# Memory attention with the decode tile second, other engine orders in the window phase, and output projections whose first three tiles are rounded by feature slice

## What is computed

```python
h = x + jnp.concatenate([out_a, out_b, out_c], axis=-1) @ lw['w_o']
h = h + memory_attend(rmsnorm(h, lw['norm_mem_g']), mem_k, mem_v, lw)

def memory_attend(hn, mem_k, mem_v, lw):
    q = rmsnorm((hn @ lw['w_mq']).reshape(B, T, MEM_HEADS, MEM_HD), lw['mem_q_norm_g'])
    s = jnp.einsum('bqhd,bkhd->bhqk', q, mem_k) * (MEM_HD ** -0.5)
    p = jax.nn.softmax(s, axis=-1)
    return jnp.einsum('bhqk,bkhd->bqhd', p, mem_v).reshape(B, T, D_MODEL) @ lw['w_mo']
```

## Time and profile before

| | us |
|---|---|
| median of the runs | 1981.98 |
| profiled execution, own time | 1981.09 |
| its span | 1979.6 |
| TensorE busy (PE) | 1853.4, 94% |
| weight loads (PEld) | 1697.4, 86% |
| VectorE busy (DVE) | 1140.2, 58% |
| ScalarE busy (ACT) | 787.6, 40% |
| GpSimd busy (POOL) | 739.6, 37% |

### The profile page before, as it was taken

How to read it: one execution, slowest core, us unless ns; L and a number is a source line. 1 busy time by engine, 2 the same in 40 slices (tenths; PEclk the granted TensorE clock), 3 DMA queues, 4 the chain that set the end, 5 groups by cost and what they waited for, 6 DMA issues and landing times. The chain is left out here.

```text
span 1979.6 us, 27880 instructions
## 1 busy us (share of the span) xinstructions
PE 1853.4 (94%) x10427; PEld 1697.4 (86%) x10427; DVE 1140.2 (58%) x1348; ACT 787.6 (40%) x1483; POOL 739.6 (37%) x652
## 2 busy tenths in 40 slices
PE   5999999989979799898997997999999999999999
PEld 4989889989958587898985786999999999988787
DVE  4225555856655511521341217887887887699995
ACT  4115663325675421411401316444444444444432
POOL 3001212015534240221201503766666666546743
PEclk9999999999989899998998998999999999999999
DMA  5111211232144230212053212222222222386544
GB/s 161 35 55 47 55 33 45 81 111 86 57 142 152 87 126 1 64 64 86 1 182 114 87 44 82 67 67 77 76 67 67 77 66 76 133 325 210 177 165 153
DMA packets 159033, 188.07 MB, mean 95 GB/s; under 512 B 13809, under 2 KB 112730, under 8 KB 158520
## 3 DMA queue, kind: packets, MB, share of 16 engines
q1 hardware_dynamic: 157156, 186.30, 28.6%
q10 hardware_dynamic: 884, 0.25, 0.1%
q0 software_dynamic: 896, 0.19, 0.1%
HBM read 151.64 MB, written 35.07 MB: 94 GB/s over the span
## 5 line engine op out<-in xcount | busy, mean ns | idle before, releaser
L3394 PE MATMUL ffn_banks<-h_parts,up_hi 128*128 128x384 f32 x1936 | 495.8, 337 | 11.5 <-POOL h_parts L3793 4.3
L3394 PEld LDWEIGHTS ffn_banks<-h_parts,up_hi 128*128 128x128 f32 x1936 | 351.6, 189 | 13.5 <-issue 8.2
L3394 PE MATMUL ffn_banks<-h_parts,up_lo 128*128 128x384 f32 x968 | 325.0, 336 | 0.0
L3789 POOL TENSOR_TENSOR up_lo<-up_raw,up_hi 128x512 fp32r<-128x512 f32 x176 | 256.7, 1474 | 139.1 <-ACT up_hi L3547 139.1
L761 PE MATMUL proj_banks<-x_hi,in_w_hi 128*128 128x384 f32 (+1 forms) x648 | 223.4, 345 | 4.2 <-DVE room L1148 4.2
L761 PE MATMUL proj_banks<-x_hi,in_w_lo 128*128 128x384 f32 (+1 forms) x648 | 218.2, 337 | 0.0
L761 PE MATMUL proj_banks<-x_lo,in_w_hi 128*128 128x384 f32 (+1 forms) x648 | 218.1, 337 | 0.0
L3394 PEld LDWEIGHTS ffn_banks<-h_parts,up_lo 128*128 128x128 f32 x968 | 183.0, 189 | 0.0
L3840 POOL TENSOR_TENSOR h_parts<-down_cells,h_parts 128x512 fp32r<-128x512 f32 x69 | 110.9, 1614 | 89.7 <-ACT h_parts L3620 89.6
L3510 PE MATMUL ffn_banks<-h_parts,up_hi 128*128 128x512 f32 x352 | 138.3, 393 | 2.5 <-DVE h L4067 1.9
L3513 PE MATMUL ffn_banks<-h_parts,up_lo 128*128 128x512 f32 x352 | 137.1, 390 | 0.0
(11 more groups left out here) (470 smaller groups left out, 3900.3 us busy)
## 6 DMA issues: line engine op xcount, KB each, us to landing
up_raw<-in_w_up SPq DMA_DIRECT2D x44, 512.0 KB, 3.8
down_cells<-in_w_down SPq DMA_DIRECT2D x58, 256.0 KB, 5.5
up_raw<-ffn_gated_rows SPq DMA_DIRECT2D x44, 320.0 KB, 5.3
ffn_gated_rows<-h SPq DMA_DIRECT2D x22, 576.0 KB
in_w_raw<-in_w_in SPq DMA_DIRECT2D x24, 512.0 KB, 3.7
up_raw<-ffn_gated_rows SPq DMA_DIRECT2D x44, 256.0 KB, 3.2
mem_k_one<-in_cache_mem_k SPq DMA_DIRECT2D x8, 1024.0 KB, 4.9
spill<-mixT SPq DMA_DIRECT2D x10, 576.0 KB, 3.8
```

Source lines behind the costliest of these rows:

```text
L3394: ins = nc.tensor.matmul(banks[:, bank, 0:TC], wt[:, j, k, :], parts[:, q, x, k, :], start=(fresh and n == 1), stop=(n == last), skip_grou ...
L3789: nc.gpsimd.tensor_tensor(w_lo[:, j], weights.full(j), w_hi[:, j].bitcast(F32), ALU.subtract).then_inc(weights.split[j], 1)
```

## The change

Three parts. Nothing is computed otherwise; instructions and waits change their places and sizes.

1. Window phase: the orders of VectorE and ScalarE. One load of ScalarE's function table goes, the copy of the transposed values stands behind the scaling of the memory rows, `exponentials(0)` behind the first two high parts, `maxima(1)` ahead of `weights_low(3)`, `copy_turned(0)` and `weights_high(3)` ahead of `exponentials(1)`, `weights_high(4)` behind `rows_out(0)`. The key lengths are inverted at i = 3, and the eight normalizations are spread over i = 3, 4 and 5.

```diff
 LENGTHS_AT = {1: (0, 1), 2: (2,), 3: (3,)}
-KEYS_AT = {5: (0, 1, 2, 3), 6: (4, 5, 6, 7)}
+FACTORS_AT = 3
+KEYS_AT = {3: (0, 1), 4: (2, 3, 4), 5: (5, 6, 7)}
...
             nc.vector.tensor_copy(k_rows[:], t_bank[:, 1:3, :]).then_inc(rows_copied, 1)
+            for f in range(2):
+                low(f)
             denominators(0)
-            for f in range(4):
-                low(f)
-            for f in range(4, KD):
+            for f in range(2, KD):
                 low(f)
             weights_low(1)
+            maxima(1)
             weights_low(3)
-            maxima(1)
             denominators(1)
...
-                if i == 4:
+                if i == FACTORS_AT:
                     refine_keys()
                 for n in KEYS_AT.get(i, ()):
...
-            nc.scalar.preload_act_table_set("natural_log_exp_and_others")
-            act.wait_ge(v_turned, 1)
-            nc.scalar.activation(v_rows[:, 0:8, :], t_bank, ACT.Copy).then_inc(v_copied, 1)
...
+            act.wait_ge(v_turned, 1)
+            nc.scalar.activation(v_rows[:, 0:8, :], t_bank, ACT.Copy).then_inc(v_copied, 1)
+            for f in range(2):
+                high(f)
             exponentials(0)
-            for f in range(4):
+            for f in range(2, 4):
                 high(f)
             weights_high(0)
             for f in range(4, KD):
                 high(f)
-            for j in range(1, 4):
+            for j in range(1, 3):
                 weights_high(j)
+            copy_turned(0)
+            weights_high(3)
             exponentials(1)
-            for j in range(4, PAIRS_FIRST):
-                weights_high(j)
             for i in range(NT):
-                copy_turned(i)
-                if i == 0:
+                if i:
+                    copy_turned(i)
+                else:
                     rows_out(0)
+                    weights_high(PAIRS_FIRST - 1)
                 for g in LENGTHS_AT.get(i, ()):
                     key_lengths(g)
                 for j in PAIRS_AT.get(i, ()):
                     weights_high(j)
                 if i + 2 < NT:
                     exponentials(i + 2)
-                if i == 4:
+                if i == FACTORS_AT:
                     key_factors()
```

```diff
...
-            sp.wait_ge(w_split, i - self.RING + 1)
+            sp.wait_ge(w_split, i - self.RING + 2)
...
-            for k in range(KD):
-                pe.wait_ge(w_split, k + 1)
+            pe.wait_ge(act_high_first, 1)
+            for half in range(2):
+                for a, w in ((a_hi, w_hi), (a_lo, w_hi), (a_hi, w_lo)):
+                    if w is w_lo:
+                        pe.wait_ge(w_split, half + 1)
+                    elif a is a_hi:
+                        pe.wait_ge(w_high, half + 1)
+                    elif half == 0:
+                        pe.wait_ge(act_split_first, 1)
+                    for t in range(together):
+                        nc.tensor.matmul(banks[:, 2 * t + half, :], a[:, t, 0, :], half_of(w[:, 0], half),
+                                         start=(a is a_hi and w is w_hi), stop=False)
+            for k in range(1, KD):
+                pe.wait_ge(w_split, k + 2)
+                pe.wait_ge(act_split_first, k + 1)
                 for n in range(2 * together):
-                    if k == 0 and n % 2 == 0:
-                        pe.wait_ge(act_split_first, n // 2 + 1)
                     products(n, k)
...
-            for k in range(KD):
+            nc.scalar.activation(a_hi[:, 0:together, 0], first_slice(0), ACT.Copy).then_inc(act_high_first, 1)
+            weights.wait(act, 0)
+            for half in range(2):
+                nc.scalar.activation(half_of(w_hi[:, 0], half), half_of(weights.at(0), half), ACT.Copy).then_inc(w_high, 1)
+            for k in range(1, KD):
+                nc.scalar.activation(a_hi[:, 0:together, k], first_slice(k), ACT.Copy).then_inc(act_high_first, 1)
                 weights.wait(act, k)
                 nc.scalar.activation(w_hi[:, k], weights.at(k), ACT.Copy).then_inc(w_high, 1)
-                if k < together:
-                    act_hi_part(k)
...
-            pool.wait_ge(w_split, 1)
+            pool.wait_ge(w_split, 2)
             for k in range(1, KD):
-                pool.wait_ge(w_high, k + 1)
+                pool.wait_ge(w_high, k + 2)
...
-                pool.wait_ge(act_high, t + 1)
+                pool.wait_ge(act_high, t - together + 1)
...
-            dve.wait_ge(w_high, 1)
-            nc.vector.tensor_tensor(w_lo[:, 0], weights.at(0), w_hi[:, 0].bitcast(F32), ALU.subtract).then_inc(w_split, 1)
-            for t in range(together):
-                dve.wait_ge(act_high, t + 1)
-                nc.vector.tensor_tensor(a_lo[:, t], act_tile(t), a_hi[:, t].bitcast(F32), ALU.subtract
-                                        ).then_inc(act_split_first, 1)
+            def low_slice(k):
+                dve.wait_ge(act_high_first, k + 1)
+                nc.vector.tensor_tensor(a_lo[:, 0:together, k], first_slice(k), a_hi[:, 0:together, k].bitcast(F32),
+                                        ALU.subtract).then_inc(act_split_first, 1)
+
+            low_slice(0)
+            for half in range(2):
+                dve.wait_ge(w_high, half + 1)
+                nc.vector.tensor_tensor(half_of(w_lo[:, 0], half), half_of(weights.at(0), half),
+                                        half_of(w_hi[:, 0], half).bitcast(F32), ALU.subtract).then_inc(w_split, 1)
+            for k in range(1, KD):
+                low_slice(k)
```

```diff
+    last = NT - 1
+    SAMPLE_AT = 1
+    tile_at = [0, last] + list(range(1, last))
...
+            for b in range(4):
+                load_k(b)
+            for b in range(2):
+                load_v(b)
+            for b in range(4, NB):
+                load_k(b)
+            for b in range(2, NB):
+                load_v(b)
+            load_next(sp)
...
+            def sample_scores(out):
+
+                for m in range(HEADS * NB + 2):
+                    if m >= 2:
+                        b, h = divmod(m - 2, HEADS)
+                        pe.wait_ge(masked_ready, b + 1)
+                        pe.wait_ge(k_copied, m - 1)
+                        for j in range(2):
+                            ins = nc.tensor.matmul(out[:, h, :], masked[:, b % 2, 2 * h + j, :], k_one_t[:, m % 2, j, :],
+                                                   start=(b == 0 and h % 2 == 0 and j == 0), stop=(b == NB - 1 and j == 1),
+                                                   skip_group_check=True)
+                        ins.then_inc(k_used, 1)
+                    if m < HEADS * NB:
+                        b, h = divmod(m, HEADS)
+                        if h == 0:
+                            pe.wait_ge(k_landed[b % 2], 16 * (b // 2 + 1))
+                        if m >= 2:
+                            pe.wait_ge(k_copied, m - 1)
+                        for j in range(2):
+                            for kt in range(2):
+                                ins = nc.tensor.transpose(o_bank[:, 4 * (m % 2) + 2 * j + kt, :],
+                                                          k_one[:, b % 2, kt, P * (2 * h + j):P * (2 * h + j) + P], C.ident[:])
+                        ins.then_inc(k_turned, 1)
...
+            def turn_rows():
+
+                pe.wait_ge(rows_copied, 1)
+                for f in range(8):
+                    ins = nc.tensor.transpose(o_bank[:, f, :], rows[:, P * f:P * f + P], C.ident[:])
+                ins.then_inc(rows_turned, 1)
...
+            def output(i):
+                t, now = tile_at[i], pT[:, i % 2]
+                if i:
+                    pe.wait_ge(out_copied, i)
                 else:
+                    pe.wait_ge(k_copied, HEADS * NB)
...
+            score(0)
+            score(1)
+            for i in range(NT):
+                turn(i)
+                if i == SAMPLE_AT + 1:
+                    turn_rows()
+                if i + 2 < NT:
+                    score(i + 2)
+                output(i)
...
+            def copy_keys():
+
+                for m in range(HEADS * NB):
+                    if m == HEADS:
+                        denominators(0)
...
+            maxima(0)
+            copy_keys()
+            maxima(1)
+            for i in range(NT):
+                if i == SAMPLE_AT + 1:
+                    copy_rows()
+                if i + 1 < NT:
+                    denominators(i + 1)
+                if i:
+                    output_copy(i - 1)
+                if i + 2 < NT:
+                    maxima(i + 2)
+            output_copy(NT - 1)
...
+                if i == SAMPLE_AT + 2:
+                    act.wait_ge(rows_turned, 1)
...
+            exponentials(0)
+            for i in range(NT):
+                if i + 1 < NT:
+                    exponentials(i + 1)
+                copy_turned(i)
...
+            for n in range(2):
+                mask(n, qT[:, :, TP:T])
+            normalize(0)
```

(9 more changed lines are left out.)

471 lines of the change are left out of this document (159 added, 312 removed).

## The result

The changed kernel takes 1946.59 us (median, 1945.3 to 1949.46) against 1982.17 for the kernel before: ratio 0.9823 (95% interval 0.9806 to 0.984), 35.6 us less by the medians, 35.1 by the ratio (3.4 either way). The forecast was 1946. The profiled execution took 1945.3 us, its span is 1943.8 us, against 1981.09 and 1979.6 before; no product was added or taken out, and TensorE's busy time fell by 11.3 us all the same, so what went is idle time and half clock. First the busy lines of the page and then the stages; after each stretch stand its length, the busy times of TensorE, its weight loads, VectorE, ScalarE and GpSimd with their counts, TensorE's granted clock, the DMA share and GB/s.

A forecast was written before the change was run, and what follows sets the result against it. TensorE was taken as the bound, busy nearly everywhere, so only its pauses and half clock could be won: 2.0 + 7.2 + 6.0 + 17.6 + 5.8 - 2.9 = 35.7 us, giving 1946 us, range 1938 to 1957.

The forecast's parts named there:

- window phase, start: Start of window phase: unit 8 sooner, new 3.8 us pause before `turn(1)`; gain 3.5 us, taken as 2.0, bounds 0 and 7.3.
- window phase, end: End of window phase: 0.8 us of the first pause, the 5.10 us pause and 2.0 us half clock go; 7.2 us.
- first projection: Start of the first output projection: first product about 1.3 us after ScalarE's start; gain 6.0 us before clock.
- memory attention: Memory attention: pauses and half clock worth 21.2 us go, new waits of 1.4, 0.3, 1.5 and 0.4; gain 17.6 us.
- second projection: Start of the second output projection: 7.7 us lost before, new loss 1.9; gain 5.8 us before clock.
- clock behind the projections' pauses: Output projections: one of the two starts is hit by half clock behind its new pause, costing 2.9 us.
- GpSimd's order and its first release are as before: Window phase start: early edits cost nothing, covered by GpSimd; units 0 to 7 still end at 587.86.
- the stall of 0.5 us at slice 1: Output projection start: weight slice 1 ready 6.0 us in but wanted at 5.5, so TensorE stalls 0.5 us.
- The split into waits and clock: Memory attention: gain divided into vanished waits (4.05, 6.12, 1.70 us among them) and avoided half clock (2.6 and 3.8 us).
- The rival of half clock in the key steps: Memory attention: key steps and value products take up to twice as long, 70 us more, 2016; chance 0.02.
- That with no new pause caught by the clock: All new pauses: none brings half clock, 3.5 instead of 2.0 at window start, no 2.9; 40.1 us, 1942; chance 0.20.
- the late keys: Attention part of a rival: value loads hold keys 4 to 6; with late window copies 8 to 13 us back; chance 0.13.

The follow-up runs named there:

- cache copy early: Changed kernel with VectorE's copy of the transposed window cache ahead of the low part of weight pair 7 instead of behind it: 1946.54 us, ratio 0.9814.
- all filled: Changed kernel plus early cache copy, tile 0 exponentials first, value loads behind keys 0 and 1, and dummy transposes in TensorE's pauses: 1939.64 us, ratio 0.9793.

## Why the prediction was right, step by step

Forecast and measured, in us; the measured ones are differences of the two profiled executions, 35.8 in all:

| term | forecast | measured |
|---|---|---|
| window phase, start | 2.0 | -0.7 |
| window phase, end | 7.2 | 6.3 |
| first projection | 6.0, less clock | 5.0 |
| memory attention | 17.6 | 17.8 |
| second projection | 5.8, less clock | 5.6 |
| clock behind the projections' pauses | -2.9 | in the two above |
| elsewhere | 0 | 1.9 |
| sum | 35.7 | 35.8 |

- **Window phase, start: the step that failed** is "GpSimd's order and its first release are as before". The exponentials of tile 0 now stood behind two high parts, the first of which waited 2.5 us for TensorE; GpSimd's first normalization came 1.1 us later from the phase's start (11.77 us in, before 10.64). It took both the new order and the longer half clock at the phase's start to make it late (above). With the exponentials put back, units 0 to 7 end 23.1 us into the phase, exactly where the earlier trace rows has them (587.86), and `turn(1)` starts 34.9 us in, where the forecast said 599.8, 35.0 us in. So the forecast's gain of 3.5 us was to be had; 1.5 us went with the late release, and 2.8 with half clock behind `turn(1)`, for which it had allowed 1.5. The pause itself, 3.2 us for 3.8, hides a second gap: nothing was taken for VectorE's steps that GpSimd held up (last section), among them the low part of pair 5, 3.4 us instead of 1.2. The low part of pair 7 itself cost the 1.2 us it was priced at. In after the held-up VectorE came to it only 0.3 us late, because pair 7 was rounded late as well (at 598.87, forecast 597.35); with the cache copy ahead of pair 7, the copy stands behind these held-up steps, and 2.08 us of pause are left.
- **Window phase, end:** mechanism and place right. The first pause shrank by 0.4 instead of 0.8 us, since the three normalizations that stand ahead of the copy take 2.9 us; the 5.10 us one went, one of 1.0 us took its place at 666.67 (the text of the forecast says 0.5, its sum takes 0.7). No copy near output 4 came late: from 613.47 to 660.00 TensorE never paused.
- **Projections:** the first product comes 1.7 and 1.5 us into the phase (1.8 and 1.6 forecast), and from there TensorE does not pause: the stall of 0.5 us at slice 1 did not come. Half clock stood behind one of the two starts, as taken, but it cost 1.3 us (C-D is 106.0 us in after and 104.7 in the runs where the clock held) and not 2.9: it lasted 3.5 us, from 679.4 to 682.9, and not the 6.8 that were taken. Without it the first projection's gain is 6.3 us.
- **Attention:** the new waits are within 0.1 us of the forecast: 1.40 for key 4 (1.5), 0.44 and a run of 1.09 for `turn_rows` (1.4 together), 0.33 for `output(2)` (0.3), 1.40 after the first transposes (1.3). The key steps, for which nothing was taken, stay at 1.30 us. The split into waits and clock was tried alone and held: 5.95 us against 6.4. The rival of half clock in the key steps is out: clock 1.00 from 911.8 to the end.
- **Elsewhere, not forecast:** the query projection, 125.84 to 123.85 us. It ends with 36 matmuls one column wide, and nearly the whole difference is in them, 6.14 us before and 4.30 after:

```profile
913.10 6.14 PE L2795 MATMUL mq_sums<-ones,mq_squares 128*128 128x1 f32 x36
902.92 4.30 PE L2592 MATMUL mq_sums<-ones,mq_squares 128*128 128x1 f32 x36
```

Before, the clock fell 2.1 us after the first of them, at 915.2, while TensorE was busy; after, 5.2 us after it, at 908.1, with the phase's end. In all 14 traces it fell 2.1 to 5.5 us after the first of these matmuls. So these 2 us are no gain of the change. The theory that the attention brings them fails as a rule: with the new attention the clock fell early as well, 2.7 and 3.0 us in (cache copy early, all filled), and D-E was 126.8 and 124.4. With the old one it fell 2.1 to 3.2 us in, five times of five; whether that is more than chance stays open. The forecast had half clock only behind pauses, and this stretch is one without.

That the sum came out to 0.1 us is therefore chance in part: misses of 2.7 and 0.9 us in the window phase were made up by 1.9 us that came unasked elsewhere and 1.7 us at the projections, where half clock had been priced too high. Of the rivals none came about in after. That with no new pause caught by the clock is nearly what the profiled run with the exponentials first shows, and of the late keys only the forecast's own one for key 4 exists (1.2 us of E-F).
